# Seven products of sums for eight in the last three FFN stages of a decoder trunk

## What is computed

```python
def _swiglu_ffn(h, w_in, w_out):            # w_in 1024 x 5632, w_out 2816 x 1024
    gu = h @ w_in
    gate, up = jnp.split(gu, 2, axis=-1)
    return (jax.nn.silu(gate) * up) @ w_out
for i in range(DEPTH):                       # DEPTH = 2
    x = x + 0.5 * _swiglu_ffn(_rmsnorm(x, ffn_norm[i, 0]), ffn_w_in[i, 0], ffn_w_out[i, 0])
    x = x + mixer(_rmsnorm(x, mix_norm[i]))
    x = x + 0.5 * _swiglu_ffn(_rmsnorm(x, ffn_norm[i, 1]), ffn_w_in[i, 1], ffn_w_out[i, 1])
```

## Time and profile before

| | us |
|---|---|
| median of 3 runs (lowest, highest) | 951.9 (951.85, 952.64) |
| span of the profiled execution | 950.0 |
| PE busy | 943.8 |
| VectorE busy | 762.9 |
| ScalarE busy | 495.2 |

### The profile page before, as it was taken

How to read it: one execution, slowest core, us unless ns; L and a number is a source line. 1 busy time by engine, 2 the same in 40 slices (tenths; PEclk the granted TensorE clock), 3 DMA queues, 4 the chain that set the end, 5 groups by cost and what they waited for, 6 DMA issues and landing times.

```text
span 950.0 us, 12305 instructions
## 1 busy us (share of the span) xinstructions
PE 943.8 (99%) x4392; PEld 778.6 (82%) x4392; DVE 762.9 (80%) x1447; ACT 495.2 (52%) x777; POOL 102.3 (11%) x94
## 2 busy tenths in 40 slices
PE   9999999999999999999999999999999999999998
PEld 7888888888978888888888888888778888888887
DVE  5778887879989887878788787877777888878782
ACT  6644353468755454444555344445778745444440
POOL 0100000068802000000000000001333100000000
PEclk9999999999999999999999999999999999999999
DMA  9876555544547636364554636353434545364521
GB/s 326 334 284 238 205 181 216 209 176 148 185 165 248 229 139 259 132 241 157 222 184 163 251 132 254 145 226 134 172 117 150 179 177 219 135 240 158 225 84 45
DMA packets 29548, 182.47 MB, mean 192 GB/s; under 512 B 3520, under 2 KB 3904, under 8 KB 9408
## 3 DMA queue, kind: packets, MB, share of 16 engines
q1 hardware_dynamic: 27360, 175.19, 48.9%
q0 software_dynamic: 2144, 6.70, 2.3%
HBM read 180.83 MB, written 1.05 MB: 191 GB/s over the span
## 4 chain that ended last, share of the span: by engine, by line
PE 98%; DMA 0%; DVE 0%; POOL 0%; ACT 0%; issue 0%; SPq 0%
PE pg L563 17%; PE pg L571 17%; PE pg L567 17%; PE acc L563 13%; PE acc L571 13%; PE acc L567 13%; PE pt L786 2%; PE pt L667 1%; PE acc L893 1%; PE pt L912 1%; DMA raw<-in_units 0%; PE acc L615 0%; PE pt L874 0%; PE acc L620 0%; PE acc L623 0%; PE pt L697 0%
## 5 line engine op out<-in xcount | busy, mean ns | idle before, releaser
L1397 DVE TENSOR_TENSOR w_lo<-raw,w_hi 128x1024 fp32r<-128x1024 f32 x304 | 356.4, 1221 | 18.2 <-ACT w_hi L985 16.9
L985 ACT CAST w_hi<-raw 128x1024 fp32r<-128x1024 f32 x314 | 311.2, 1046 | 20.7 <-DMA raw<-in_units 20.6
L563 PE MATMUL pg<-w_hi,a_hi 128*128 128x512 f32 x720 | 282.6, 392 | 0.0
L571 PE MATMUL pg<-w_hi,a_lo 128*128 128x512 f32 x720 | 280.3, 389 | 0.0
L567 PE MATMUL pg<-w_lo,a_hi 128*128 128x512 f32 x720 | 280.2, 389 | 0.0
L1497 DVE STREAM_TRANSPOSE mix<-hs 32x128 f32<-32x128 f32 x592 | 179.2, 303 | 8.9
L563 PEld LDWEIGHTS pg<-w_hi,a_hi 128*128 128x128 f32 x720 | 135.2, 188 | 28.7 <-issue 1.4
L571 PEld LDWEIGHTS pg<-w_hi,a_lo 128*128 128x128 f32 x720 | 135.2, 188 | 28.1
L567 PEld LDWEIGHTS pg<-w_lo,a_hi 128*128 128x128 f32 x720 | 135.3, 188 | 27.4
L1030 ACT ACTIVATE hs<-pg,rstd 128x256 f32<-128x256 f32 x80 | 37.8, 475 | 160.0 <-PE pg L571 160.0
L1489 DVE SCALAR_TENSOR_TENSOR hs<-pg,rstd,hs 128x256 f32<-128x256 f32 x80 | 38.2, 483 | 101.7 <-ACT hs L1030 101.7
(11 more groups left out here) (161 smaller groups left out, 745.7 us busy)
## 6 DMA issues: line engine op xcount, KB each, us to landing
raw<-in_units SPq DMA_DIRECT2D x157, 1024.0 KB, 5.2
diags<-in_conv_diags SPq DMA_DIRECT2D x8, 512.0 KB, 4.2
raw<-in_units SPq DMA_DIRECT2D x12, 256.0 KB, 7.0
diags<-in_conv_diags POOLq DMA_DIRECT2D x4, 512.0 KB, 4.8
gain<-in_ffn_norm POOLq DMA_DIRECT2D x3, 512.0 KB, 4.8
xs<-in_x SPq DMA_DIRECT2D x4, 256.0 KB, 8.3
gain<-in_mix_norm POOLq DMA_DIRECT2D x2, 512.0 KB, 5.5
xg<-in_conv_b_in POOLq DMA_DIRECT2D x2, 512.0 KB, 4.1
```

The lines of the kernel that those rows point to most:

```text
L563: mm = pe.matmul(dst[j], stat_hi, m_hi, start=first, stop=False)
L571: mm = pe.matmul(dst[j], stat_lo, m_hi, start=False, stop=last)
L985: nc.scalar.copy(w_hi[n % RING][:, cols], raw[n % RAW][:, cols]).then_inc(hi_done, 1)
L1397: nc.vector.tensor_tensor(w_lo[n % RING][:, cols], raw[n % RAW][:, cols], w_hi[n % RING][:, cols].bitcast(F32), ALU.subtract).then_inc(lo_ ...
```

## The change

In the stages 2, 3 and 5 (`FAST`) chunks 1 to 10 are taken as five pairs of 512 gate and 512 up columns. Chunk 0 stays as it is.

- A plain pair (pairs 1, 3 and 5) has four units of 24 matmuls: gate columns for both input halves into `pg`, up columns into `pt`; and two second units.
- A pair by sums (pairs 2 and 4) has seven products of 12 matmuls in place of the eight. Four weight sums of 128 x 2048 are made in place on VectorE (`sum_weights`), the products are combined by a copy on ScalarE (`kept_sum`) and five VectorE operations of 512 columns. Nine forms are rounded and rested for six loaded units. Sums of the input are made once a stage: ScalarE copies the turned input from PSUM (`keep`), four VectorE sums, four roundings and four rests of 512 columns, kept in one of the six `w_hi`/`w_lo` places, so that five are left for weights.
- Weights are rounded and rested in one instruction of 2048 columns instead of two halves, from the fourth form of these stages on. Three more `raw` places lie in the buffers of the convolution and the attention; a written-out plan says which load goes where and waits for what.
- Hidden values of a pair are turned by one VectorE block transpose over all 128 partitions, and then change partitions by 16 transfers of 32 partitions x 1 KB (512 bytes for chunk 0), issued from ScalarE's queue (`move`). PE transposes no hidden values in these stages.
- The loops over chunks are written out.

```diff
+MODES = ('plain', 'blocks', 'plain', 'blocks', 'plain')
+ORDER = [("b11", "b21", "b12", "b22", "wa")] + [("b11", "u1", "u2", "wa", "b22", "u3", "b21", "u4", "wb") if mode == "blocks" else
+                                               ("b11", "b21", "wa", "b12", "b22", "wb") for mode in MODES[1:-1]] \
+    + [("b11", "b21", "b12", "b22", "wa", "wb", "wc", "wd")]
...
@@ tensor
+                def product(n, stationary, bank, first):
+                    unit_ready(n)
+                    hi, lo = hi_of(n), lo_of(n)
+                    for k in range(4):
...
+                        mm = pe.matmul(bank, s_hi, hi[:, cols], start=first and k == 0, stop=False, skip_group_check=not first)
+                        if k == 0:
+                            mm.then_inc(unit_begun, 1)
+                        pe.matmul(bank, s_hi, lo[:, cols], start=False, stop=False, skip_group_check=not first)
+                        mm = pe.matmul(bank, s_lo, hi[:, cols], start=False, stop=k == 3, skip_group_check=not first)
+                    mm.then_inc(product_ready, 1)
...
+                def by_sums_pair(d):
+                    g, q = pair_index(s, d), sums_before(s, d)
+                    pe.wait_ge(gates_done, 2 * g - 1)
+                    product(form_at(s, d, "b11"), x_block(0, 0), pg[:, 0, :], True)
+                    pe.wait_ge(mixed_lo_done, 4 * i + 4)
...
+                        pe.wait_ge(pair_gated, 2 * g - 1)
+                    product(form_at(s, d, "u1"), mixed(2), pt[:, 0, :], True)
...
+                        pe.wait_ge(pair_gated, 2 * g)
+                    product(form_at(s, d, "u2"), mixed(1), pt[:, 1, :], True)
+                    seconds(2 * d - 3)
+                    pe.wait_ge(combined_done, 5 * q + 1)
+                    product(form_at(s, d, "b22"), mixed(3), pt[:, 0, :], False)
+                    pe.wait_ge(combined_done, 5 * q + 2)
+                    product(form_at(s, d, "u3"), mixed(0), pt[:, 1, :], False)
+                    pe.wait_ge(kept_done, q + 1)
+                    product(form_at(s, d, "b21"), x_block(0, 1), pg[:, 0, :], False)
+                    pe.wait_ge(combined_done, 5 * q + 4)
+                    product(form_at(s, d, "u4"), x_block(1, 1), pt[:, 1, :], False)
+                    seconds(2 * d - 2)
...
@@ scalar
+                def move(d):
+                    n = 8 * 32 if d else 4 * 32
+                    act.wait_ge(blocks_turned, turn_index(s, d) + 1)
+                    if d:
+                        act.wait_ge(h_lo_done, FCH * f + 2 * d - 1)
+                    for q in range(4):
+                        for b in range(4):
+                            nc.scalar.dma_start(hidden_moved[b * 32:(b + 1) * 32, q * T:q * T + n],
+                                                gated_by[q * 32:(q + 1) * 32, b * n:(b + 1) * n]).then_inc(pair_moved, 16)
...
+                def by_sums_pair(d):
+                    b, n = u + PAIR_AT[d], u + PAIR_AT[d + 1]
+                    round_form(b + 4)
+                    round_form(b + 5)
+                    keep_first(d)
+                    hidden_pair(2 * d - 3)
+                    round_form(b + 6)
+                    hidden_pair(2 * d - 2)
+                    round_form(b + 7)
+                    round_form(b + 8)
+                    round_form(n)
+                    round_form(n + 1)
+                    round_form(n + 2)
+                    gates_of(d, 0)
+                    round_form(n + 3)
+                    gates_of(d, 1)
+                    round_form(n + 4)
+                    move(d)
+                def plain_pair(d):
+                    b, n = u + PAIR_AT[d], u + PAIR_AT[d + 1]
+                    round_form(b + 5)
+                    if d > 1:
+                        hidden_pair(2 * d - 3)
+                        hidden_pair(2 * d - 2)
+                        round_form(n)
+                    else:
+                        hidden_pair(0)
+                    gates_of(d, 0)
+                    gates_of(d, 1)
+                    round_form(n + 1)
+                    round_form(n + 2)
+                    round_form(n + 3)
+                    move(d)
...
+                round_form(u + 4)
+                round_form(u + 5)
+                round_mixed(2, 1)
...
+                gate(0)
+                round_form(u + 6)
+                move(0)
...
@@ vector
+                def turn_blocks(d):
+                    k = 4 if d else 2
...
+                    nc.vector.transpose(gated_by[:, 0:k * T].rearrange("p (a m n) -> p a m n", a=4, n=32),
+                                        wide[:, 0:k, :, :].rearrange("p k t (a n) -> p a (k t) n", a=4)).then_inc(blocks_turned, 1)
...
+                def by_sums_pair(d):
+                    b, n = u + PAIR_AT[d], u + PAIR_AT[d + 1]
+                    rest_form(b + 3)
+                    sum_weights(d, 3)
+                    rest_form(b + 4)
+                    second_less(d)
+                    hidden_pair(2 * d - 3)
+                    rest_form(b + 5)
+                    both_less(d)
+                    rest_form(b + 6)
+                    rest_form(b + 7)
+                    hidden_pair(2 * d - 2)
+                    rest_form(b + 8)
+                    first_up(d)
+                    rest_form(n)
+                    last_up(d)
+                    rest_form(n + 1)
+                    gate_up(d, 0)
+                    rest_form(n + 2)
+                    last_gate(d)
+                    rest_form(n + 3)
+                    gate_up(d, 1)
+                    turn_blocks(d)
+                def plain_pair(d):
+                    b, n = u + PAIR_AT[d], u + PAIR_AT[d + 1]
+                    rest_form(b + 4)
+                    if d > 1:
+                        rest_form(b + 5)
+                        hidden_pair(2 * d - 3)
+                        hidden_pair(2 * d - 2)
+                    rest_form(n)
+                    sum_weights(d + 1, 0)
+                    if d == 1:
+                        hidden_pair(0)
+                    sum_weights(d + 1, 1)
+                    rest_form(n + 1)
+                    sum_weights(d + 1, 2)
+                    rest_form(n + 2)
+                    gate_up(d, 0)
+                    gate_up(d, 1)
+                    turn_blocks(d)
...
+                rest_form(u + 4)
+                sum_x(0, region(1, 1), region(1, 0), region(1, 1), ALU.subtract)
...
+                rest_form(u + 5)
+                rest_mixed(2, 1)
...
+                gated_first()
+                turn_blocks(0)
```

More of the change, by code:

```diff
@@ new lines, with by_sums @@
+assert MODES == ("plain", "blocks", "plain", "blocks", "plain")
+PAIR_AT = [None] + [2 + sum(len(forms) for forms in ORDER[:d]) for d in range(DOUBLES + 1)]
+FAST_FORMS = PAIR_AT[-1]
+SECOND_AT = [PAIR_AT[1 + d] + k for d in range(DOUBLES) for k, name in enumerate(ORDER[d]) if name[0] == "w"]
+def by_sums(d):
+    return MODES[d - 1] == "blocks"
+BEFORE = [None] + [sum(by_sums(e) for e in range(1, d)) for d in range(1, DOUBLES + 2)]
+READY = [None] + [sum(BLOCKS if by_sums(e) else 2 * TT for e in range(1, d)) for d in range(1, DOUBLES + 2)]
@@ L104 @@
+UNIT0, LOAD0 = PLAN.form0, PLAN.load0
+FORMS, LOADS = len(PLAN.forms), len(PLAN.loads)
 CONV, ATTN = 1, 4
@@ L720, in ffn @@
[L720 to L726 removed]
+                    first_unit(n, 0, banks)
+                    first_unit(n + 1, 1, banks, {4 if s == 0 else 3: lambda: turn_gated(0)} if first and by_tensor(s, 0) else {})
+                    hidden_ready(c - 1)
@@ L1188, in conv @@
                     silu(kt)
-                for w in range(1, 4):
+                for w in range(1, 3):
                     tick(u + 2 * chunks + w)
@@ L1526, in chunk @@
-                def chunk(c, i, skip_first):
+                tick(u)
+                hidden(0)
+                tick(u + 1)
+                gated(1)
+                tick(u + 2)
+                tick(u + 3, lambda: hidden(1))
+                tick(u + 4)
+                for c in range(2, FCH):
                     n = u + 2 + 3 * (c - 1)
-                    if not skip_first:
-                        tick(n, i)
-                    tick(n + 1, i)
-                    gated(c, i)
+                    tick(n)
+                    tick(n + 1)
+                    gated(c)
@@ L1871, in pairs, with wide @@
         return w.reshape(-1, 2, P, D).transpose(0, 2, 1, 3).reshape(-1, P, UNIT)
-    out = np.empty((UNITS, P, UNIT), np.float32)
+    def wide(w):
+        w = w.reshape(2, 4, P, 2, F)[..., CH:].reshape(2, 4, P, 2, DOUBLES, BANK)
+        return w.transpose(4, 3, 0, 2, 1, 5).reshape(DOUBLES, 2, 2, P, UNIT)[:, ::-1]
+    out = np.empty((LOADS, P, UNIT), np.float32)
     for s, (kind, layer, which, chunks) in enumerate(STAGES):
-        u = UNIT0[s]
-        if kind == "ffn":
+        u = LOAD0[s]
+        if s in FAST:
+            first, second = halves(ffn_w_in[layer, which]), pairs(ffn_w_out[layer, which])
+            out[u:u + 2] = first[0]
```

(13 more changed lines are left out.)

613 lines of the change are left out of this document (483 added, 130 removed).

## The result

| | before | after |
|---|---|---|
| median of the runs, us | 952.3 (951.9 to 952.9, 4 runs) | 1095.5 (1095.2 to 1097.9, 4 runs) |
| span of the profiled run, us | 950.0 | 1096.1 |
| ratio of the times, 95% interval | | 1.151 (1.149 to 1.153) |
| PE busy / idle in the span, us | 943.8 / 6.2 | 962.5 / 133.6 |
| mean granted clock | 0.999 | 0.936 |

The change makes the kernel 15% slower; the prediction said 3%, 983 us, within 949 to 1018. A stage is counted from the first update of the residual to the next stage's first, on VectorE's timeline; the second and the fifth, which the change doesn't touch, hardly move (99.3 and 99.2; 111.2 and 111.8).

A forecast was written before the change was run, and what follows sets the result against it. PE, the matmul engine, was taken as the bound: 951.9 less 17.7 us saved gives 934.2; with 49.2 us of pauses, +31.5 net, the profile's span of 950.0 becomes 981.5, and 1.9 more makes 983 us, range 949 to 1018.

The forecast's parts named there:

- 17.7 us: PE's saving over three stages: 16.3 us from fewer matmuls and 1.4 us from dropped PE transposes, 5.9 us a stage.
- The walk: Step-by-step timing of queues through a changed stage; PE's pauses of 16.9, 16.9 and 15.4 us sum to 49.2 us.
- (c): Pair 1's turn, issues and queued roundings make PE wait 7.3 us for the second hidden unit.
- The second rival: The burst price of an issue holds, 0.46 to 0.50 us: time 1016 to 1025 us; chance 0.15 for 1006 or more.
- I take 0.33 us each, 5.3 us for 16; ... the upper 0.50: Assumed price of a turn's transfer issues on ScalarE's queue, from SyncE issue rows; lower bound 0.08 us or a little less.
- (a): After chunk 0's turn, issues and form 7 delay the first hidden rest: PE pauses 2.0 us.
- (b): VectorE's sums, rests and gating come late for a bank that PE wants at 48.0: pause 3.2 us.
- (d): Turns of pairs 3, 4 and the last: late by 1.7, 1.2 and 1.5 us, the last not in the final stage.
- The clock: Half pace after pause (c) would cost 2.4 us per ten matmuls, three times 7 us in all; left out of the sum.
- The loads... costed at nothing: Same number of loads into six places for three; no form waits for its load; small transfers add 8.3 MB to 182.
- The loops written out: Loops over chunks unrolled: no row shows an instruction fetch that PE waits for; 0 to 1 us.
- The first rival: Issues are cheap, 0.05 to 0.12 us; VectorE alone is late, 5.3 to 6.5 us a stage; 950 to 954 us; chance 0.19.

The follow-up runs named there:

- kept_warm_2: Changed kernel with spare matmuls (28, 50, 28, 20 and 24) ahead of five second-half units a stage, into banks nobody waits for; 1083.6 us, ratio 1.139.
- narrow_moves: Changed kernel with all sixteen transfers of each turn issued, each carrying an eighth of its columns (32 of 256); 1091.6 us.
- dram_two: Changed kernel with turned blocks sent through memory by SyncE, one write and four reads a turn, two pairs by sums; 986.4 us, ratio 1.036.
- whole_moves: Changed kernel with four transfers of 128 partitions a turn on ScalarE's queue in place of sixteen of 32, same bytes; 992.8 us.
- sync_moves: Changed kernel with all sixteen transfers of each turn issued by SyncE and none by ScalarE; 1044.7 us, ratio 1.097.
- half_moves: Changed kernel with eight of the sixteen transfers of each turn left out; 1004.1 us.
- split_moves: Changed kernel with eight transfers of each turn on ScalarE's queue and eight on SyncE's, at the same time; 1007.9 us.
- all_plain: Changed kernel with all five pairs of each stage by the eight products, turning and sixteen transfers kept; 1060.4 us.

## Why the prediction was wrong

**What held.** PE was the bound and its 17.7 us were saved. The transfers landed after 1.9 us (median), for the 2.0 assumed. VectorE's prices were right: a whole form 2.29 us busy, the block transpose 1.25 us, as the timeline above shows. A whole form on ScalarE took 1.90 us busy and 1.80 to the next one's start (356.75 to 358.55), for 1.81. The walk named all six places where PE would wait in the third and fourth stage, with (c) the longest; in the sixth stage it had no last pause, and PE waited there 5.9 us. The second rival's direction, dearer issues, was the right one.

**The term that was mis-sized** is "I take 0.33 us each, 5.3 us for 16; ... the upper 0.50". An issue is 0.61 us, sixteen are 10.2. Each pause behind a burst then grows by 10.2 - 5.3 = 4.9 us. In the fourth stage, put beside the walk:

| pause | predicted | with 4.9 more | measured |
|---|---|---|---|
| (a) | 2.0 | 6.9 | 7.1 |
| (b) | 3.2 | 3.2 | 1.4 |
| (c) | 7.3 | 12.2 | 11.9 |
| (d) | 1.7, 1.2, 1.5 | 6.6, 6.1, 6.4 | 6.7, 5.1, 7.5 |
| sum | 16.9 | 41.4 | 39.7 |

Three stages of 24.5 us more are 73.5 of the 112.5 us by which the time was missed. The choice went wrong where it said "the nearest are SyncE's hardware-queue issues": every row had memory at one end, and none a transfer within SBUF. They bounded a different operation, and 0.50, the crowded price of the same wrong kind, was no upper bound; a row that differs in kind needs room above it, which this range did not leave. The second rival's own pauses, redone, come to 79.5 us at 0.46 and not to 82, so 1014 for 1016, which changes nothing here. The 50 ns of the Trainium skill (DMA: Bandwidth & Descriptors, Anatomy of one DMA — SWDGE (gpsimd) path), which stand there for another path, were rightly kept out of the sum: measured here, 0.61 us.

**The clock** was "left out of the sum". PE worked 33 us longer for it. kept_warm_2 took 26 of these away and the time fell by 12; the other 14 had only taken the place of waiting. The earlier trace rows had the price about right, 2.2 us a pause (1.6 to 3.0) for the 2.4 said, but it was paid behind fifteen pauses and not behind the three of (c).

**"The loads... costed at nothing"** was partly wrong. In the third stage the last pause is 12.0 us for 7.5 in the fourth, with the DMA engines full of the next stage's loads; this stage is 6.6 us longer than the fourth, and still 2.6 us with an eighth of the transfers' bytes (narrow_moves: 230.3 and 227.7). The runs with fewer transfers show the same as landings of 12.6 us (dram_two) and 15.5 us (whole_moves). The transfers add 8.7 MB by the profile, for the 8.3 of the text.

**The loops written out** cost nothing that the traces show, and 0 to 1 us had been said. The first stage's residual update does come 2.2 us later than before (188.3 us for 186.2). But PE is 1.4 us late within the first 14 us, where it waits for the rounding of the first loads, and the rest has come by 53 us, where the loop only begins in the kernel before. From there to the end of the stage it falls no further behind.
```profile
9.25 0.70 PE L840 MATMUL acc<-w_hi,a_hi 128*128 128x512 f32 x2 [2.17 <-ACT w_hi L1401]
```
In the other kernels with the same code this stage ends between 0.8 us early and 2.3 us late, and in each of them the whole shift is there by that point. The 0.6 us of the fifth stage arise in its first 4 us; it has no loop in either kernel.

**The first rival** (cheap issues) is borne out as mechanism: without transfers VectorE alone is late by 5.4 us a stage, for 5.3 to 6.5 in the text. Even a perfect transfer would have left next to nothing of the 5.9 us saved.

**What stays open.** With the right price the walk's pauses are 49.2 + 73.5 = 122.7 us and the measured ones 124.7, but that agreement is partly chance: the walk has PE at full pace, and where it was kept there, the span was 1081.2 us and not the walk's 981.5 + 73.5 = 1055.0. Of these 26.2 us, 3.3 are the crowding of that kernel's third stage (227.5 us for the fourth's 224.2) and 2.3 its first stage; 20.6 are not settled. The kernels with a bare walk on record came out later than it, too: sync_moves by 11 us, half_moves by 22, split_moves by 26, all_plain by 31, the slow clock included; no run separates whether the rest is its small waits left out, late forms, or one stage's lateness handed to the next.

## What to carry to other kernels

Price a DMA issue by a row with the same two ends; where there is none, measure it alone before you build on it, and count the instructions, not the bytes. Many small transfers on a queue that also computes are paid twice: by who waits for them, and by all that stands behind them. Before moving a wait earlier in a queue, write down what is queued behind it; twice here a mended pause came back at the next such place. And a saving on the bounding engine stays only where its operands were early before.

## What the runs showed of the hardware

- A transfer with both ends in SBUF takes 0.59 us to issue on SyncE's queue and 0.61 to 0.62 on ScalarE's (medians), with 4 KB to 128 KB, 32 or 128 partitions; loads and stores of memory take 0.33 us, reads into 32 partitions 0.43.
- Two queues issued at the same time and hardly slowed each other (4.96 and 5.29 us for eight each, 5.00 alone).
- A write of 512 KB issued behind four loads of 1 MB landed after 12.6 us; the least of its line is 2.0, the median 2.6.
- Copies of 32 partitions x 256 values between partitions take ScalarE 0.43 us each; the 128x1024 block transpose takes VectorE 1.25 us.
- Behind the changed kernel's fifteen pauses of 5.0 to 12.0 us the granted clock was 0.50, and the next 7 to 14 matmuls ran at half pace, 1.6 to 3.0 us lost each time. The loss didn't grow with the pause: 3.0 us behind one of 6.7, 1.6 behind one of 12.0.
- Behind shorter pauses half pace sometimes came and sometimes didn't: in half_moves a pause of 3.12 us was followed by it (clock 0.50) and one of 3.13 us was not (1.00); in sync_moves one of 1.9 us was (0.61 and less).
